# Starting offsets of the moving operands in a streaming-encoder block on one core

## The reference

```python
x = x + 0.5 * swiglu(rmsnorm(x, ffn1_norm), ffn1_w_gu, ffn1_w_down)   # width 2816
x = x + token_mixing(rmsnorm(x, mix_norm), w_in, ...)   # 4 recurrent heads + 512 conv channels, then @ w_out
x = x + cross_attention(rmsnorm(x, xa_norm), rmsnorm(mem, mem_norm), wq, wkv, wo)   # 4 heads, 256 memory tokens
x = x + 0.5 * swiglu(rmsnorm(x, ffn2_norm), ffn2_w_gu, ffn2_w_down)
return rmsnorm(x, final_norm)
```

## Time and profile before

| | |
|---|---|
| median of three runs | 1103.45 us |
| the profiled execution's own time | 1100.7 us |
| its span, first to last instruction | 1098.9 us |
| granted TensorE clock, mean | 0.998 |
| PE busy | 1083.4 us, 99% |
| PE weight loads busy | 951.3 us, 87% |
| VectorE, ScalarE, GpSimd busy | 638.4, 525.8, 441.0 us |

### The profile page before, as it was taken

The page is one execution under the profiler, slowest core; times in us unless marked ns, Lnnn a source line. Parts: engine busy times, 40 slices in busy tenths (PEclk is TensorE's granted clock), DMA queues, the critical chain, the costliest instruction groups (busy, mean ns, idle before and its releaser), DMA issues.

```text
span 1098.9 us, 17317 instructions
## 1 busy us (share of the span) xinstructions
PE 1083.4 (99%) x6328; PEld 951.3 (87%) x6328; DVE 638.4 (58%) x944; ACT 525.8 (48%) x738; POOL 441.0 (40%) x546
## 2 busy tenths in 40 slices
PE   9999999999999999999999999999999999999997
PEld 7889999988888888787789888888899999888886
DVE  7887777572223668978477134466977777531012
ACT  6445555542223554664366443354555555633231
POOL 0000000486665445346448883163010000585550
PEclk9999999999999999999999999999999999999999
DMA  7277775333333121222323442122576675333212
GB/s 244 78 213 198 192 201 172 116 115 99 112 104 106 58 96 58 77 77 78 119 67 121 164 162 78 39 77 77 168 209 186 185 190 172 116 115 113 98 58 77
DMA packets 49458, 136.89 MB, mean 125 GB/s; under 512 B 4736, under 2 KB 11008, under 8 KB 49280
## 3 DMA queue, kind: packets, MB, share of 16 engines
q1 hardware_dynamic: 43888, 118.90, 31.5%
q0 software_dynamic: 4320, 15.73, 8.6%
q10 hardware_dynamic: 1200, 1.57, 0.4%
HBM read 134.09 MB, written 2.10 MB: 124 GB/s over the span
## 4 chain that ended last, share of the span: by engine, by line
PE 52%; POOL 25%; issue 21%; DVE 1%; POOLq 0%; DMA 0%; ACT 0%; DVEq 0%; SPq 0%; ACTq 0%
POOL wl L528 25%; PE bank L1629 8%; PE bank L1631 8%; PE bank L1630 8%; PE bank L1734 4%; PE bank L1735 4%; PE bank L1736 4%; PE score L1734 3%; PE score L1735 3%; PE score L1736 3%; PE o_bank L1734 1%; PE o_bank L1735 1%; PE o_bank L1736 1%; PE bank L1690 1%; PE bank L1694 0%
## 5 line engine op out<-in xcount | busy, mean ns | idle before, releaser
L528 POOL TENSOR_TENSOR wl<-raw,wh 128x256 fp32r<-128x256 f32 x512 | 414.7, 843 | 314.6 <-ACT wh L562 271.3
L562 ACT ACTIVATE wh<-raw 128x1024 fp32r<-128x1024 f32 x120 | 125.7, 1053 | 137.7 <-PE bank L1631 135.6
L1629 PE MATMUL bank<-xh,wh 128*128 128x512 f32 x456 | 183.0, 401 | 0.5 <-DVE V L1509 0.5
L1631 PE MATMUL bank<-xh,wl 128*128 128x512 f32 x456 | 178.5, 391 | 0.0
L1630 PE MATMUL bank<-xl,wh 128*128 128x512 f32 x456 | 178.4, 391 | 0.0
L542 POOL DMA_DIRECT2D raw<-w_all x30 | 26.1, 869 | 317.8 <-DMA raw<-w_all 317.8
L1629 PE MATMUL bank<-zr,wh 128*128 128x512 f32 (+1 forms) x374 | 141.0, 377 | 0.0
L1630 PE MATMUL bank<-zr,wh 128*128 128x512 f32 (+1 forms) x374 | 140.8, 377 | 0.0
L1631 PE MATMUL bank<-zr,wl 128*128 128x512 f32 (+1 forms) x374 | 140.8, 377 | 0.0
L1013 DVE SCALAR_TENSOR_TENSOR x<-bank,x 128x512 f32<-128x512 f32 (+1 forms) x31 | 21.3, 687 | 160.5 <-PE bank L1631 160.1
L1629 PEld LDWEIGHTS bank<-xh,wh 128*128 128x128 f32 x456 | 85.6, 188 | 20.3 <-issue 2.4
(11 more groups left out here) (325 smaller groups left out, 2554.4 us busy)
## 6 DMA issues: line engine op xcount, KB each, us to landing
raw<-w_all SPq DMA_DIRECT2D x200, 512.0 KB, 3.3
raw<-w_all POOLq DMA_DIRECT2D x30, 512.0 KB, 5.4
zf<-w_all SPq DMA_DIRECT2D x30, 256.0 KB, 4.4
x<-x_t SPq DMA_DIRECT2D x8, 256.0 KB, 6.2
out_t<-x SPq DMA_DIRECT2D x8, 256.0 KB, 2.6
raw<-w_all SPq DMA_DIRECT2D x6, 256.0 KB, 6.1
memf<-mem_t ACTq DMA_DIRECT2D x1, 1024.0 KB, 5.5
raw<-w_all ACTq DMA_DIRECT2D x2, 256.0 KB, 4.1
```

The lines of the kernel that those rows point to most:

```text
L528: ins = nc.gpsimd.tensor_tensor(wl[:, slot, two], raw[:, slot, two], wh[:, slot, two].bitcast(f32), SUB)
L562: nc.scalar.activation(wh[:, slot, :], raw[:, slot, :], ACT.Copy).then_inc(hi_ready, 1)
L1629: nc.tensor.matmul(out_, a[0], b_[0], start=first, stop=False)
L1631: return nc.tensor.matmul(out_, a[1], b_[0], start=False, stop=last)
```

## The change

Three constants are changed and one helper is added; the code that uses them is otherwise as before.

```diff
 EVEN = 96
-HID_AT = HID * T + EVEN
+HID_EVEN = 48
+HID_AT = HID * T + 128 + HID_EVEN
...
-        xh, xl = at_column(xh_both, 0), at_column(xl_both, 0)
+        xh, xl = at_column(xh_both, 32), at_column(xl_both, 32)
...
+        def high(z, first, n=1):
+            return z[:, first * T + HID_EVEN:(first + n) * T + HID_EVEN]
+
...
             if j < NF:
-                return tiles(zr, j), hidden(zr, j)
-            return tiles(zr, NF + 2 * (j - NF)), tiles(zr, NF + 2 * (j - NF) + 1)
-        sb("room_cat", [128, EVEN])
+                return high(zr, j), hidden(zr, j)
+            return high(zr, NF + 2 * (j - NF)), high(zr, NF + 2 * (j - NF) + 1)
+        sb("room_cat", [128, EVEN - 16])
...
-                    nc.scalar.activation(tiles(zr, 2 * n, 2), hidden(zf, 2 * n, 2), ACT.Copy).then_inc(hid_hi, 2)
+                    nc.scalar.activation(high(zr, 2 * n, 2), hidden(zf, 2 * n, 2), ACT.Copy).then_inc(hid_hi, 2)
...
-                                     tiles(zr, 2 * n, 2).bitcast(f32), SUB).then_inc(hid_lo, 2)
+                                     high(zr, 2 * n, 2).bitcast(f32), SUB).then_inc(hid_lo, 2)
```

## The result

Over 20 executions of each kernel the changed one takes 1108.92 us in the median and the one before 1102.86: ratio 1.0066, 95% interval 1.0055 to 1.0076. The change costs 6 to 7 us; 1086 was forecast. Of the changed kernel's executions 14 lie between 1108.2 and 1109.2 us and five between 1113.6 and 1114.2; one of 1555.6 us, at a granted clock of 0.65, is left out. The profiled one, 1113.84 us, is of the second group; what sets it apart is in its trace, and has to be told from the rest.

The account below looks back on a forecast made before the run. TensorE without gaps was taken as the bound, matmul count times pace. Terms -16.5 and -2.8 us, plus 1.5 hidden in the mixer, made -17.8 us; against the median 1103.45 that gave 1086, range 1080 to 1091.

Parts of the forecast that it names:

- What bounds the kernel: Whole kernel: TensorE is busy 99% of 1098.9 us, so time is the number of matmuls times their pace.
- That the offset counts: All matmuls: the moving operand's offset modulo 512 sets the pace, 226.7 ns at 0 against 232.9 at 192 with 512 columns.
- Which end?: Choice between 220.0 and 233.3 ns for 512 columns at the new offsets; the lower was taken weakly, -16.5 us.
- (a): xh and xl outside the prepared copy, 0 to 128: 1056 matmuls, 576 in the mixer, +-7.0 us.
- (b): Feed-forward values, high and low, 0 to 320: 990 matmuls of 512 columns and 132 of 256, +-6.6 us.
- (c): Merged heads, 0 to 448: 384 matmuls; together with pTh +-2.9 us.
- (e): Value projection: xh stationary at 128 and mh at 448, 96 matmuls each, moving side at 0; tells distance from absolute place.
- The cover in the mixer: Mixer: of 3.8 us gained by 576 matmuls, 1.5 us would be lost in waits for VectorE and ScalarE.
- The products of quarters must keep 113.3, since their moving side does not move: Feed-forward products of quarters, 256 columns at 192: pace stays at 113.3 ns in the profile after.
- All dearer: Rival: offset 0 is the good rhythm, all 2478 matmuls cost a step more, +13.7 us, 1117; chance 0.27.
- mixed or nothing: Rival: families move differently or not at all, 1092 to 1114, such as 1110 if only offset modulo 128 counts; chance 0.31.

Follow-up runs that it names:

- m1_pace: Separate kernel without the block: 22 runs of 96 matmuls, moving operand and weights at different offsets; 226.7 to 233.3 ns with 512 columns, 113.3 to 120.0 with 256.
- m2_fine: Separate kernel without the block: runs of 72 matmuls at 16-byte steps, and high and low parts at different places; none under 226.7 or 113.3 ns.
- e_hid: Kernel before with only the feed-forward values moved from 0 to 320: 1105.26 us, ratio 1.0017.
- e_best: Kernel before with all 16 prepared-copy groups computed as two halves of 256 columns, and mh, ml, kTh, kTl at 192: 1101.51 us, ratio 1.0012.
- e_cat: Kernel before with only the merged heads and what lies behind them moved from 0 to 448: 1105.48 us, ratio 1.0019.
- e_hidcat: The change without x: feed-forward values at 320, heads and what lies behind at 448, x at 0: 1106.30 us, ratio 1.0034.
- m3_handed_on: Separate kernel without the block: twelve unbroken sequences, 512 columns at 0 or 128, then 512 and 256 at 192; the 256 took 113.3 or about 117.8 ns.
- e_256: Kernel before with feed-forward values, heads and what lies behind the heads moved to 256, x at 0: 1101.99 us, ratio 0.9995.
- e_last: Kernel before with only the four last prepared-copy groups of each feed-forward computed as two halves of 256 columns: 1100.78 us, ratio 0.9984.

## Why the prediction was wrong

**What bounds the kernel: right.** PE without gaps; the time is count times pace. The result is pace, less 1 us that the mixer hides.

**That the offset counts: right.** The two pages of the Trainium skill that spoke against it don't hold for these matmuls. The Trainium skill, "TensorE: Matmul & The Clock Gate", section "Back-to-back issue gap", has a formula that gives 215.8 ns at every offset. It calls that the gap of a single matmul, which the prediction left out, and gives about 131 ns for a sustained stream of 512 columns. m1_pace has none under 226.7 and three values. The same page of the Trainium skill says in "Step-by-step: what each phase is for" that loading the next weights takes no read bandwidth from the running matmul. The runs disagree in so far as the distance between these two reads alone is worth 6.7 ns a matmul. The Trainium skill, "SBUF — State Buffer", section "SBUF: two separate sides", lets TensorE wait for nobody; the trace agrees as far as other engines go (226.6 and 226.9 ns in the earlier trace rows), and says nothing of TensorE's own two reads, where the distance counts.

**"Which end?": wrong, and this turned the sign.** The prediction took 220.0 ns at all three new offsets. The reasoning was that offset 0, with both reads starting at the same place, was a collision that any other offset would relieve, since 256 columns gain at 192. m1_pace shows that this holds for 256 columns and is the other way round for 512: distance 0 modulo 256 is their best, and none of the offsets tried in m2_fine beats it. What failed is the step from the 256 columns to the 512: the term of -6.67 ns a matmul, 16.5 us in all, was +2.2 to +6.7 ns. The upper bound, 233.3, was right for 128 and 448; for 320 the truth was 228.9, which no row of before had. The evidence against was in the earlier trace rows and in the rival's words: the only other offset with 512 columns was worse, and unsettled steps took 231. A row of the same width should have weighed more than a rule from another width.

**The sizes.** (a) was +-7.0: the settled pace at 128 is 232.1 ns more often than 233.3, so 1056 matmuls are worth 5.4 ns each, 5.7 us, of which about 1 is hidden in the mixer (below); like for like the runs have 3.8 to 3.9, the traces 4.6. (b) was +-6.6 and is +2.2 by the stage marks of the change and of e_hid and by the pace, less 0.6 for its halves of 256 columns. (c) with pTh was +-2.9; the stage marks have 1.1 + 1.2, and the keys give back some 0.8 of the 2.8 that all 256 columns were to give, since `mh` went at 115.7 ns in the mean, 192 x 4.3 ns. The table's 113.3 for distance 192 was not reached there (e_best had 117.8), so inside the block the distance alone does not fix the pace. (e) was the test of distance against place, and distance it is; its price the prediction left at nothing. In the mixer's value projection only the stationary side moved, to a distance of 128: the undisturbed steps of its 96 matmuls have a mean of 228.0 ns before and 232.3 after, 0.4 us in all. In cross-attention the stationary `mh` moved to a distance of 64, and the stretch between the same two starts goes from 23.9 to 24.2 us, at 229.3 ns in the mean for 227.0. In e_cat and e_hidcat the same 96 matmuls take 231.2 ns, which the distance does not explain (before and after, instructions of `mh`: durations min/median/max, first and last start).

```profile
L1629 PE MATMUL bank<-wh,mh x32: 389/389/396, 624.2 to 648.1; 128*128 128x512 f32 x32
```
```profile
L1633 PE MATMUL bank<-wh,mh x32: 392/394/396, 634.3 to 658.5; 128*128 128x512 f32 x32
```

**The cover in the mixer: right, with the sign turned.** The prediction let 1.5 us of a 3.8 us gain vanish in waits for VectorE and ScalarE. Windows of PE over the whole mixer stage, before and then after:

```profile
348.33:543.20 194.87, 189.55 (x935) 1.00 0.23 76
```
```profile
355.95:552.74 196.79, 192.43 (x935) 1.00 0.23 75
```

The same 935 matmuls are busy 2.9 us longer (x's undisturbed steps have a mean of 227.8 ns before and 232.5 after, which is 2.7 us for 576, and the value projection adds 0.4), and PE's gaps shrink from 5.3 to 4.4 us. A slower PE waits less, so 1.0 of the 2.9 us is hidden, and the stage grows by 1.9. The foreseen share, 1.5 of 3.8, is near it.

**Not foreseen at all.** "The products of quarters must keep 113.3, since their moving side does not move" failed in the profiled execution (117.9) and in five of 19 by their times. The prediction itself had said that a stretch "finds a rhythm", but took this for something that ends with the stretch.

**The rivals.** "All dearer" had the sign and the mechanism, offset 0 as the good one, at twice the price (1117). The measured time lies where "mixed or nothing" had 1110, by another rule than modulo 128: all three families went up, one of them by a third of a step.

## What to carry to other kernels

Where PE has no gaps, measure the start-to-start pace for each width and each distance between moving and stationary operand in a small kernel of its own before moving anything: it took one run here to fill the table that the forecast guessed at. A pace seen at one width did not even give the sign for the other here. And leave a family that stands at the best value of that table alone; a worse rhythm can be handed on to stages that nobody touched.

## What the runs showed of the hardware

- Float32r matmuls that alternate with weight loads go at 226.7, 228.9 or 233.3 ns for 512 columns and at 120.0, 117.8, 118.6 or 113.3 ns for 256, by the distance of the two starts modulo 256 bytes (0, 64, 128, 192), at a granted clock of 1.00 (m1_pace). In steps of 16 bytes the paces form no smooth curve (m2_fine). At distance 128 a second rhythm has 232.1 ns (m3_handed_on).
- The best distance for one width is among the dearest for the other: of the four multiples of 64, 0 is the best for 512 columns (226.7) and the worst for 256 (120.0), and 192 the best for 256 (113.3) and, with 128, the worst for 512 (233.3).
- A run of matmuls depends on the one before it: 256 columns at 192 go at 113.3 or 117.8 ns by what ran 17 us earlier (11 of 12 sequences by the rule, one not), through a stretch whose mean pace is the same in both.
- After a wait of 2.1 us in the mixer the granted clock fell to 1.2 GHz for eight matmuls, and the stage took 2.7 us longer (e_256, e_hid). In e_last PE had a longest wait for `kdT` of 2.1 us too, with the clock at 1.00, so the wait alone does not decide it.
- A slower PE has a part of its loss hidden where it waits for others: 1.0 of 2.9 us in the mixer.
- Open: what in the reads makes the steps of 2.2 and 6.7 ns, and what decides between the two rhythms of distance 128 (cycle of seven, 232.1 ns; 229 and 238 in turn, 233.3) at its start. The float32 matmul as a break changed the odds (8 of 11 fast against 0 of 4), and no run tells why.
